# Fifty-two expert slots of tile 0 among the attention heads of tiles 2 to 4, with two more landing places and each tile's choices in four turns

## The reference, cut to what matters

```python
q = (hb @ w_pq).reshape(t, P_HEADS, 2, P_QDIM // 2)
sc = jnp.einsum('thpd,hpkd->thpk', q, keys)
sv, si = lax.top_k(sc, P_TOPK)
cand = sv[:, :, 0, :, None] + sv[:, :, 1, None, :]
cv, ci = lax.top_k(cand.reshape(t, P_HEADS, 256), P_TOPK)
eidx = take_along_axis(cidx, ci)
gate = softmax(cv)
act = gelu(einsum('thkd,td->thk', u_tab[eidx], hb))
out = einsum('thk,thkd->td', gate * act, v_tab[eidx])
```

## Time and profile before

| | us |
|---|---|
| median of 3 runs (5096.21 to 5101.77) | 5101.31 |
| the profiled execution | 5101.03 |
| its span | 5099.2 |
| PE busy | 3987.9 (78%) |
| DVE busy | 2904.9 (57%) |
| ACT busy | 1637.7 (32%) |
| POOL busy | 1522.9 (30%) |

### The profile page before, as it was taken

One profiled execution on the slowest core, in us unless ns is written; L12 is line 12 of the kernel. 1 busy time (PEld: TensorE's weight loads), 2 busy tenths in 40 slices (PEclk: granted clock), 3 DMA queues, 4 the chain that ended last, 5 costly groups with the idle time before them and its releaser, 6 DMA issues.

```text
span 5099.2 us, 61250 instructions
## 1 busy us (share of the span) xinstructions
PE 3987.9 (78%) x19854; PEld 1568.1 (31%) x19854; DVE 2904.9 (57%) x6339; ACT 1637.7 (32%) x4803; POOL 1522.9 (30%) x1453
## 2 busy tenths in 40 slices
PE   5989988998886666666679899889988756666666
PEld 3555564232321111111134556633323211111111
DVE  3541464666787666554445414546667876665544
ACT  0222143333333333333322211433333333333333
POOL 0210002333444444333312100023333344443332
PEclk7989999999986777666679899999998867677666
DMA  7113305999999999999951133069999999999998
GB/s 280 48 51 124 132 26 210 408 413 383 421 415 393 421 421 421 421 421 421 421 195 48 51 128 136 18 239 407 411 396 421 394 399 421 421 421 421 421 421 355
DMA packets 223883, 1577.22 MB, mean 309 GB/s; under 512 B 25744, under 2 KB 27984, under 8 KB 35920
## 3 DMA queue, kind: packets, MB, share of 16 engines
q0 software_dynamic: 184320, 1342.26, 63.9%
q1 hardware_dynamic: 39248, 231.06, 12.1%
HBM read 1569.94 MB, written 3.28 MB: 309 GB/s over the span
## 4 chain that ended last, share of the span: by engine, by line
PE 40%; DMA 35%; DVE 16%; issue 4%; ACT 3%; DVEq 2%; SPq 0%; POOL 0%; ACTq 0%; POOLq 0%
DMA arena<-in_experts,arena 28%; PE ps L759 14%; PE ps L993 8%; DVE sq L1471 7%; DMA front<-in_experts,arena 6%; PE ps L944 4%; PE ps L969 3%; PE ps L896 2%; PE ps L957 2%; PE ps L921 2%; PE ps L908 1%; DMA arena<-in_weights 1%; DVE negm L1365 1%; DVE arena L1197 1%; PE ps L825 1%
## 5 line engine op out<-in xcount | busy, mean ns | idle before, releaser
L993 PE MATMUL ps<-arena 64*64 64x512 f32 x9088 | 1645.1, 810 | 834.4 <-ACT arena L1134 788.3
L732 POOL DMA_INDIRECT arena<-in_experts,arena x1136 | 1228.6, 1081 | 2824.6 <-PE ps L993 1738.0
L1471 DVE CUSTOM_DVE_ANT_0 sq<-arena 128x1024 f32<-128x1024 f32 x1136 | 1393.2, 1226 | 990.2 <-DMA arena<-in_experts,arena 926.5
L993 PEld LDWEIGHTS ps<-arena 64*64 64x64 f32 x9088 | 326.3, 162 | 2040.9 <-issue 2012.8
L1128 ACT ACTIVATE arena<-arena 128x1 f32<-128x1 f32 x1280 | 259.2, 203 | 1978.7 <-DVE arena L1471 1977.9
L759 PE MATMUL ps<-arena 128*128 128x512 f32 (+3 forms) x1920 | 787.7, 558 | 1.9 <-ACT arena L1042 0.9
L1134 ACT ACTIVATE arena<-ident,arena 128x128 f32<-128x128 f32 x1280 | 513.9, 401 | 91.6 <-issue 3.3
L759 PEld LDWEIGHTS ps<-arena 128*128 128x128 f32 x1920 | 353.2, 190 | 416.1 <-issue 377.7
L1130 ACT ACTIVATE arena<-arena 128x1 f32<-128x1 f32 x1280 | 376.8, 294 | 92.4 <-issue 5.6
L969 PE MATMUL ps<-arena 128*128 128x256 f32 (+1 forms) x1024 | 331.3, 466 | 3.1 <-issue 2.3
L993 PE MATMUL ps<-front,arena 64*64 64x512 f32 x1152 | 200.1, 770 | 90.2 <-ACT arena L1134 90.1
(11 more groups left out here) (158 smaller groups left out, 3005.7 us busy)
## 6 DMA issues: line engine op xcount, KB each, us to landing
arena<-in_weights SPq DMA_DIRECT2D x182, 1024.0 KB, 7.4
arena<-in_experts,arena POOLq DMA_INDIRECT x1136, 21.5
arena<-mod_rows SPq DMA_DIRECT2D x30, 512.0 KB, 6.9
arena<-in_weights SPq DMA_DIRECT2D x8, 576.0 KB, 4.6
arena<-in_keysT SPq DMA_DIRECT2D x4, 1024.0 KB, 9.8
arena<-in_weights SPq DMA_DIRECT2D x4, 768.0 KB, 4.2
arena<-in_weights SPq DMA_DIRECT2D x6, 512.0 KB, 3.5
front<-in_experts,arena POOLq DMA_INDIRECT x144, 15.2
```

What stands on the lines that cost most here:

```text
L732: pool.indirect_dma_start(out=ring[BUF[n]], out_offset=None, in_=ins["experts"], in_offset=bass.IndirectOffsetOnAxis(ap=index(t)[:, slot:s ...
L993: last = MM(acc[h][to:to + 64, c * 512:(c + 1) * 512], diag[n % 4][lo:lo + 64, lo:lo + 64], ring[BUF[n]][lo:lo + 64, D + c * 512:D + (c + ...
L1471: V.tensor_tensor_reduce(out=sq[:], in0=ring[BUF[n]][:, 0:D], in1=h2_of_slot(n), scale=1.0, scalar=0.0, op0=ALU.mult, op1=ALU.add, accum_o ...
```

## The change

- The attention of tiles 2 to 4 is cut after its first six heads. Those six are mixed with the first turn of tile 0 (`mixed`). The other 42 heads go on the line, at places -1 to 49. The slots start at place 0, so 52 slots of tile 0 (FRONT) run among heads.
- merge and route of tiles 2 to 4 go to places 52 to 240 (before: -3 to 248).
- Every turn ends in its own tkx and tkg of 32 columns, and ends four places ahead of the slots it serves (turn n at 32n-30 to 32n-4; the eighth at 32n-14). No choices lie inside route.
- The first 52 slots use buffers 4, 11, 12 and 13 only. 11 is a free stretch of the arena. 12 and 13 are two of the three weight places: the loads of gate (0,1) and proj (0,0) of tiles 2 to 4 wait on SP until the last front slot in them is used. rows2, keys and g2 stand behind them on SP. Slot 52's gather waits for the last head's output.
- The first 56 slots of a layer compute Gelu as x(1+tanh(...))/2 with Square, Copy, Identity, Tanh, Identity ahead of the diagonal (six ACT instructions, before three); their gates are halved beforehand.
- The slots' sums need two banks (0 and 1): both 512-column halves go to one bank on different partitions. Front heads use banks 2 and 3 for O, so that s, PT and qT have the pairs 4 and 6, and pair 2 only while no O is held there.
- Small moves: places of values and contexts in the arena, the diagonal matrices of the front.

```diff
+FRONT = 52
+TANHS = FRONT + 4
 def turn(l, t, u):
-    return [("tk2", l, t, u, j) for j in range(6)]
+    return [("tk2", l, t, u, j) for j in range(6)] + [("tkx", l, t, u), ("tkg", l, t, u)]
...
+def mixed(items, more):
+    per, given, s = len(more) / len(items), 0, []
+    for i, it in enumerate(items):
+        s.append(it)
+        n = int(per * (i + 1) + 1e-6)
+        s += more[given:n]
+        given = n
+    return s + more[given:]
...
-        s += attention(l, (2, 3, 4), choose(l, 0)) + [("rows2", l, 1), ("keys", l, 1), ("g2", l, 0)]
+        heads = attention(l, (2, 3, 4))
+        bare = heads.index(("s", l, 2, 0, 6))
+        s += mixed(heads[:bare], turn(l, 0, 0))
         line = Line()
         line.slots(l)
-        line.spread(8, 100, choose(l, 1))
-        line.spread(-3, 248, pieces(merge(l, 1) + route(l, 1, 2)))
-        line.spread(258, 340, choose(l, 3))
+        line.spread(-1, FRONT - 3, heads[bare:])
+        line.put(FRONT - 2.9, [("rows2", l, 1), ("keys", l, 1), ("g2", l, 0)])
+        line.spread(FRONT, 240, pieces(merge(l, 1) + route(l, 1)))
+        for n in range(1, 4 * NT):
+            line.spread(32 * n - (30 if n != 8 else 14), 32 * n - 4, turn(l, *divmod(n, 4)))
         if l == 0:
             line.spread(400, 630, mod_items(1))
-        line.spread(350, 450, choose(l, 4))
...
     elif _k == "O":
         if _it[4] == 1:
-            _take(_it, _it[3], 1)
+            _b = _it[3] + 2 * (_it[2] > 1)
+            _take(_it, _b, 1)
+            _rows |= {_b} - {0, 1}
     elif _k in PAIR:
-        _take(_it, min((4, 6) if _open else (2, 4, 6), key=lambda b: max(_used[b:b + 2])), 2)
+        _take(_it, min((b for b in (2, 4, 6) if not _rows & {b, b + 1}), key=lambda b: max(_used[b:b + 2])), 2)
...
-NBUF = 11
+NBUF = 14
...
-    _there = [b for b in range(NBUF) if b not in RELEASE or (...)]
+    _there = [4, 11, 12, 13] if _s < FRONT else [b for b in range(11) if b not in RELEASE or (...)]
...
-        acc = [ps[:, 2 * h:2 * h + 2, :].rearrange("p a n -> p (a n)") for h in range(2)]
+        acc = [ps[:, h, :] for h in range(2)]
...
             def load(n):
+                if n in HELD:
+                    sp.wait_ge(slot_used, HELD[n] + 1)
...
                         if t == 0 and slot == 0:
+                            pool.wait_ge(*ready("sink", l, 1))
+                            pool.wait_ge(*full("pq", l, 0, 15))
+                        if t == 0 and slot == FRONT:
                             pool.wait_ge(*ready("om", l, NT - 1, 1))
...
-                            last = MM(acc[h][to:to + 64, c * 512:(c + 1) * 512], diag[n % 4][lo:lo + 64, lo:lo + 64],
-                                      ring[BUF[n]][lo:lo + 64, D + c * 512:D + (c + 1) * 512], ...)
+                            last = MM(acc[h][to:to + 64, :], diag(n)[lo:lo + 64, lo:lo + 64],
+                                      row_in(n)[lo:lo + 64, D + c * 512:D + (c + 1) * 512], ...)
...
+                    if by_tanh(n):
+                        A(of(cube), of(dots), ACT.Square, scale=GELU_B ** 0.5)
+                        A(of(share), of(dots), ACT.Copy, scale=g)
+                        act.drain()
+                        A(of(inner), of(cube), ACT.Identity, scale=of(dots), bias=of(dots))
+                        act.drain()
+                        A(of(gel), of(inner), ACT.Tanh, scale=GELU_A)
+                        act.drain()
+                        A(of(wts), of(gel), ACT.Identity, scale=of(share), bias=of(share))
```

More of the change, by code:

```diff
@@ L116, in turn @@
 def turn(l, t, u):
-    return [("tk2", l, t, u, j) for j in range(6)]
+    return [("tk2", l, t, u, j) for j in range(6)] + [("tkx", l, t, u), ("tkg", l, t, u)]
 def choose(l, t):
-    return [i for u in range(4) for i in turn(l, t, u)] + [("tkx", l, t), ("tkg", l, t)]
+    return [i for u in range(4) for i in turn(l, t, u)]
 def attention(l, tiles, among=()):
@@ L175, in route @@
         s += [("sc", l, gid, q - 1)] if 1 <= q <= 16 else []
-        if q % 4 == 1 and q > 1 and early is not None:
-            s += turn(l, early, q // 4 - 1)
-    return s + ([("tkx", l, early), ("tkg", l, early)] if early is not None else [])
+    return s
 GROUPS = {0: (0, 1), 1: (2, 3, 4)}
@@ L225, in cost @@
     return {"mod": 7.0, "hT2": 1.2, "g": 1.76, "p": 1.76, "mT": 1.2, "o": 1.76, "pq": .5 * n, "sc": .25 * n,
[L226 removed]
+            "n2r": 2.0, "n2": 1.5, "s": 1.3, "PT": 1.0, "O": 1.9, "qT": 1.3, "ob": .6, "rT": .6, "gap": 6.0, "tk2": 1.5, "tk1": 1.0}.get(k, 0.1)
 AFTER = {"g": 1.0, "p": 1.0, "o": 1.0, "n2r": 1.0, "n2": 1.0, "pq": 1.0, "sc": .8, "mod": 1.0}
@@ L437 @@
     _l, _s = divmod(_n, NT * SLOTS)
-    _there = [b for b in range(NBUF) if b not in RELEASE or (_s >= 6 and PLACE[RELEASE[b](_l)] < PLACE[("Emm", _n - 6)])]
+    _there = [4, 11, 12, 13] if _s < FRONT else [b for b in range(11) if b not in RELEASE or (_s >= 6 and PLACE[RELEASE[b](_l)] < PLACE[("Emm", _n - 6)])]
     BUF.append(min(_there, key=lambda b: _last[b]))
@@ L449 @@
 FINAL_IN = {(l, b): max(n for n in range(NSLOT) if BUF[n] == b and ETILES[n // SLOTS][0] == l) for l in range(L) for b in range(NBUF)}
+LENT, HELD = [], {}
+for _l in range(L):
+    _k = LOAD_NO[_l, 1, ("gate", 0, 0)]
+    assert LOADS[_k + 1:_k + 3] == [(_l, 1, ("gate", 0, 1)), (_l, 1, ("proj", 0, 0))]
+    LENT.append(SPACE[_k + 1:_k + 3])
+    for _j in range(2):
+        HELD[_k + 1 + _j] = max(n for n in range(NSLOT) if BUF[n] == 12 + _j and ETILES[n // SLOTS] == (_l, 0))
 for _e, (_l, _t) in enumerate(ETILES):
-    assert PLACE[("tkg", _l, _t)] < PLACE[("E", SLOTS * _e)]
+    for _u in range(4):
+        assert PLACE[("tkg", _l, _t, _u)] < PLACE[("E", SLOTS * _e + 32 * _u)]
 def build(nc, ins, outs):
@@ L533, in build @@
         cross = at(20480, D)
-        diag = [at(21504 + P * r, P) for r in range(4)]
+        diag = lambda n: at(21504 + P * (n % 4), P) if n % (NT * SLOTS) >= FRONT else ar(HT0 + D + P * (n % 4), P)
         index = lambda t: zt(t)[:, 1536:1664].bitcast(U32)
@@ L557, in build @@
         esum = take(8)
-        dots, gel, wts = (take(16) for _ in range(3))
+        dots, gel, wts, cube, inner, share = (take(16) for _ in range(6))
         assert _e[0] <= HT0 + D
         ps = ctx.enter_context(nc.psum_tensor("ps", [P, 8, 512], F32))
-        acc = [ps[:, 2 * h:2 * h + 2, :].rearrange("p a n -> p (a n)") for h in range(2)]
+        acc = [ps[:, h, :] for h in range(2)]
         fps = ps[:, :, :].rearrange("p a n -> p (a n)")
@@ L663, in _ @@
                     sp.wait_ge(*ready("om", l, (1, NT - 1)[c], 1))
+                    if c:
+                        sp.wait_ge(slot_used, max(n for n in range(NSLOT) if BUF[n] == 11 and ETILES[n // SLOTS][0] == l) + 1)
                     for copy, who in ((2, 1),) if c else ((0, 0), (1, 1)):
@@ L1112, in _ @@
                 elif kind == "tkx":
-                    t = item[2]
-                    act.wait_ge(*ready("tk2", l, t, 3, 5))
-                    out(A(gate(t), gate(t), ACT.Exp))
+                    t, u = item[2:]
+                    act.wait_ge(*ready("tk2", l, t, u, 5))
+                    g = gate(t)[:, 32 * u:32 * u + 32]
+                    out(A(g, g, ACT.Exp))
                 elif kind == "ex":
@@ L1121, in _ @@
                         act.wait_ge(*full("sw", *ETILES[e - 1]))
-                    A(cross[0:64, 0:512], acc[1][0:64, 512:D], ACT.Copy)
-                    out(A(cross[64:128, 0:512], acc[0][64:128, 512:D], ACT.Copy))
+                    A(cross[0:64, 0:512], acc[1][0:64, :], ACT.Copy)
+                    out(A(cross[64:128, 0:512], acc[0][64:128, :], ACT.Copy))
                 elif kind == "Ea":
@@ L1133, in _ @@
                         act.wait_ge(slot_used, n - 3)
-                    A(diag[n % 4], ident[:], ACT.Copy, scale=wts[:, c:c + 1]).then_inc(diag_done, 1)
+                    A(diag(n), ident[:], ACT.Copy, scale=wts[:, c:c + 1]).then_inc(diag_done, 1)
         @block.vector
```

69 lines of the change are left out of this document (44 added, 25 removed).

## The result

The changed kernel takes **5140.3 us** (median of 4, 5139.1 to 5143.8) against 5101.5 of the kernel before beside it (median of 4, 5096.2 to 5102.9): 1.0078 of its time, 95% interval 1.0066 to 1.0091, slower by 0.8%. The profiled execution's span is 5141.9. The forecast was 5067; rival B at half the heads gave 5139. The first maximum of tile 2 is the first row maximum of a layer's 48 heads; "the front" is places 0 to 52, the 52 slots that run among 42 of them.

A forecast was written before the change was run, and what follows sets the result against it. Transfers alone bound a layer's last 400 slots; PE, then DVE, bound the stages after the front. Per layer 33 + 198 + 6 + 372 + 260 = 869 against 888.7 and 883.1, saving 20 and 14: 5067 us, range 4985 to 5145.

The forecast's parts named there:

- rival B: Front: with two PSUM pairs, slots' E and Ea delay each head; 234 us at half the heads, 5139 in all; chance 0.17.
- the stretch of 52 slots with 42 heads: Places 0 to 52: PE has 178 us of work, taken as 90% busy, so 198; bounds 181 and 288.
- B's sign: What would show rival B: PE idle behind line 1081 for over 40 us in the front.
- The start: Six heads and turn 0: first gather issued after 25.4 us, landing 7, so the first slot's dot at 33.
- place 52: Handover after the front: slot 52's gather and the gate load wait; 6 us, bounds 0 and 15.
- g, p, o: Places 52 to 160: PE bounds with 366 us of work against 330 of transfers; 372 us.
- route: Places 160 to 240: DVE bounds with 254 us of work; 260 us, bounds 248 and 280.
- places 240 to 639: Slots after route, to the layer's end: transfers as before, so no change.
- the table loads: Late turns: 14 more pairs a layer, 36 us on ACT, hidden; none before slot 56, then two a turn.
- A (gaps close): Emm fills PE's gaps among heads, DVE packs route: 827 us a layer, 4983 us in all; chance 0.17.
- C (the ring of four): Front landings near 12.1 us (stretch 223), or place 52 at 15 with route 268: within 10 of 5101; chance 0.12.
- D (one bank in turn): Slot matmuls writing one bank no longer overlap: 0.85 us more on 160 slots a layer, +272, about 5340; chance 0.04.

The follow-up runs named there:

- e3: The kernel before, with the heads of tiles 2 to 4 held to the two PSUM pairs 4 and 6; 5210.7 us.
- e9: e5 plus each head's s and PT on one bank pair by parity, PT's copy before the next Exp, O in bank 2, ob/rT in bank 3; 5077.3 us.
- e1: The changed kernel, with Gelu of a layer's first 56 slots replaced by plain Tanh, three ACT instructions a slot instead of six; 5106.6 us.
- e6: The changed kernel, with Square, the gate's share and the cubic on DVE, only Tanh and Identity left on ACT ahead of the diagonal; 5125.4 us.
- e2: The changed kernel, with the front slots' dot product on DVE over 64 of 1024 columns; 5134.6 us.
- e10: The changed kernel with the diffs of e9 and e6 together; 5067.4 us.
- e5: The changed kernel, with each front head's PT placed beside its s instead of in the list's plain proportion; 5121.2 us.
- e13: The changed kernel, with the first turn of tile 2 at places 221 to 236 instead of 242 to 252; 5140.9 us.
- e14: e10 with e13's move of tile 2's first turn; 5059.7 us (median of 4), 0.9915 of the kernel before.
- e7: The kernel before with only the change's turns, merge and route at -3 to 240, no slots among heads; 5139.3 us.

## Why the prediction was wrong

**The step that failed is the stretch of 52 slots with 42 heads.** "Undisturbed that loop is s 1.4, maximum 1.0, Exp 1.1: 3.5 with handovers, under PE's 4.2 a head", and from it 90% of PE busy: 198. The loop's length was right, 3.63 in e3. Two things were wrong in its use. I compared it with PE's time for a head and its slot as if the rest of that time ran beside it; but O, qT, ob and rT pass through the same banks, so with two pairs heads alone need 4.3 us each (e3, at its clock of 0.86). And I held "DVE mostly idles when s ends" against rival B, though the queue that mattered was ACT's: a slot's instructions there take 2.03 us (764.01 to 766.04; 1.9 forecast) and stand ahead of Exp or of PT's copy. Measured 241.2 and 241.6 instead of 198. The pace is 5.5 us a head (257.5/47), over the 5.1 from which I had said rival B decides. B gave 234 and 5139. Its mechanism is what happened in two of its three parts: the pairs' part is shown by e3 and e9, ACT's by e1 and e6, but DVE's (E before the maximum) is not seen in e2. That its time came within 2 us of the measured one is luck: "half the heads" was a guess, the part of E is in it, and a front 7 and a start 6 us too short are cancelled by 12 too many for places 52 to 240. (42 heads of 6.8 are also 286, not 288.) B's sign, PE idle behind Exp over 40 us, did not come as named either: PE is idle 44 us in all, and its weight loads wait 20.5 us for Exp and 26.7 for the copy of PT.

**The clock was taken as near 1.** PE's 178 us of work were 197 at 0.91. It went together with the waits: in e10 the work is 177 to 180 at 0.98. Of the 42 us between the changed kernel's front and e10's in layer 0, 20 are PE's busy time and 22 its idle time.

**The start,** 33 forecast, took 39.2: the last index stands at 687.4, 33.1 us after the first head, where I had 25.4. I had added up DVE's work without a wait; DVE waits three times for s before that index, 8.0 us in all, as its timeline shows:

```profile
668.71 0.96 DVE L1429 TENSOR_REDUCE negm<-ps 128x1 f32<-128x768 f32 x1 [1.02 <-PE ps L947]
678.76 0.96 DVE L1429 TENSOR_REDUCE negm<-ps 128x1 f32<-128x768 f32 x1 [5.11 <-PE ps L947]
683.76 0.96 DVE L1429 TENSOR_REDUCE negm<-ps 128x1 f32<-128x768 f32 x1 [1.91 <-PE ps L947]
```

PE runs there at 0.74, and s takes up to 2.93 us. The banks are not the cause: with e10's banks the way from the first maximum to place 0 is 31.1 and 31.2, as here. It is shorter, 27.7 to 29.6, only where the clock in it was 0.84 or 0.85: in one layer each of e2, e5 and e13, which have the changed kernel's banks, and in one layer of e9 and both of e14. The first gather then landed in 5.8 us (687.72 to 693.5, less than the 7 I took).

**Right:** place 52 and g, p, o, 378 forecast, 374 and 375 measured; route, 260 against 252 and 251; places 240 to 639, "no change", within 2.2 us; the table loads. Groups of ACT in the changed kernel, their count, busy time and mean:

```profile
L1192 ACT ACT_TABLE_LOAD x38 | 48.8, 1283 | 0.7
L1167 ACT ACT_TABLE_LOAD x36 | 46.2, 1283 | 0.6
```

74 against 18 at the same two places in the kernel before (8 of them in the earlier trace rows), 72 us more, on an ACT that is busy 37% there. They are hidden: the stage is longer by 2.2 us in layer 0 and shorter by 1.2 in layer 1. Summed from the first head, 39.2 + 241.2 + 374.0 + 252.1 = 906.5 against my 869; twice the difference of 37.5 is 75, and 5067 + 75 = 5142.

**A cost that stands in the sums without its name:** the turns. I counted their busy time in 372 and 260 and those stages came out near, but nowhere said what splitting the choices costs against the kernel before. e7 shows 33 to 37 us for it together with the shorter route: 15 in the heads of tiles 2 to 4, most of the rest by place 304. How that rest divides between the three normalisations more per tile and the packing of route into 80 places was not tried.

**The other rivals.** A (gaps close): PE busy 82%, no. C (the ring of four): the median landing is 5.8 us in this stretch and DVE waits 9.0 us in all for rows; no. (Its sum was off: with 223 for the stretch it gives 5117, 16 above the kernel before and not within 10 of it.) D (one bank in turn): the slot's eight records still take 1.09 as in the earlier trace rows; no.

**The forecast's model and e9, e10.** The model had the whole Gelu on ACT, as e9 has it: 210.5 and 207.8 against 198, and 5077.3 against 5067. So dealing the banks out otherwise takes away most of the miss, not all. e10, with the cubic on DVE, takes 199.5 and 202.5 and 5067.4; that this is the forecast's own number is partly luck, since ACT has 120 us there and not 172, and the start is still 6 us longer than forecast. Moving the slots does bring time once the loop is cut: e10 is 72 us below e7, which has the turns and no moved slots. The kernel before with e9's banks was not run, so part of the 72 may be had without moving a slot; by an estimate from the earlier trace rows that part is at most about 41, since PE is idle only 20 us a layer in those heads.

## What to carry to other kernels

When a change takes a buffer away from a loop, write down the whole circle through what is left (who fills it, who frees it, and everything that stands ahead of the freeing instruction in its queue), and compare that with the time per round; an engine's busy share doesn't show it. Dealing banks out by fixed role and parity, with the freeing copies early in their queue, was worth 44 us here at the same instruction count (e9 against e5), and 63 together with PT's place beside s. And test each part of a composite change alone: here a part that looked like housekeeping cost 33 us, nearly the whole loss of the change.
